# Softmax attention by pairs of heads: the minimum taken in the pass that adds the bias, and the 1/sum applied by a diagonal matrix in the turning product

## The chip, the cores and the metric

The kernel runs on one core of a Trainium2 chip. The metric is the time of one launch in microseconds of the device, lower is better. One core has a matrix engine (TensorE, "PE" in the profile, with its weight loads as "PEld"), a vector engine (VectorE, "DVE"), a scalar engine (ScalarE, "ACT"), GpSimd ("POOL") and a queue engine (SyncE, "SP") that issues the transfers. TensorE writes its products to PSUM, eight banks of 512 float32 per partition. All data here are float32.

## The reference, cut to what matters

The network has three blocks one after the other over a sequence of 512 tokens of width 1024. Two of them hold an attention that the change touches. In both, eight heads of 64 channels attend, and what is computed per head is

```
s = (q . k) * 64**-0.5 + bias          # bias: mask of chosen keys, or position table and window
p = exp(s - max(s)) / sum(exp(s - max(s)))
o = p @ v
```

In the first block (`dsa_sparse_attention`) a query may use 128 keys that an index score selects: the bias is 0 or -1e30, the same for every head. In the second (`na_attention`) a query of a 64 wide grid sees a window of neighbours (logits with a position table `rpb`, outside the window -1e30) and 256 context tokens without a bias:

```
s_loc = einsum(q * 64**-0.5, k_band) + bias ; s_loc = where(col_valid, s_loc, -1e30)
s_ctx = einsum(q * 64**-0.5, k_ctx)
p = softmax(concat([s_loc, s_ctx]))
```

## The kernel before, in words

The program is a row of blocks; in each, every engine has its own list of instructions, and semaphores order them. `Line` records an instruction of the vector or scalar engine and waits for its end before the next. `project` runs the tiles of a matrix product and, between them, what `Beside` has been given: `tensor_beside`, `scalar_beside` and `vector_beside` hold parts that each engine carries out behind the tile of that number (a number with a half: in the middle of that tile, on TensorE only).

`PairAttention` works on 16 pairs. A pair is two heads (a = 0, 1, partitions 0 to 63 and 64 to 127) by one block s of 128 queries, j = 0..3 outside and s = 0..3 inside. Step i of each engine is:

- TensorE (`tensor`): the score products of pair i+1 (`score`, L1542), which wait until both biased copies of pair i have left PSUM (`softened`) and the plain columns too; then the turning of pair i-2, head 0 (`turn`, L1553): its probabilities, 128 queries by `cols` keys, are transposed in blocks of 128 by 128 into one shared set of PSUM banks; then the products with the values of pair i-3 (`values`, L1567); then the turning of pair i-2, head 1, which needs the banks back (`copied`).
- VectorE (`vector`): for each head the copy `S = -scale * scores - bias` (L1594); for each head the minimum over the row of S (L1599); then for both heads of pair i-1 the reciprocal of the sum (L1606) and the probabilities times it, in place (L1607). Every fourth pair `close` takes the finished output (L1745 or L1936).
- ScalarE (`scalar`): `scale_plain` of pair i+1 (L1621: the columns without a bias, second block only); then for each head the copy of the turned probabilities of pair i-2 from PSUM (L1636) and the exponential of pair i with its sum (L1640), which waits for the minimum (`taken_max`).

In the first block (`dsa_attention`) block s has 128(s+1) keys, all with a bias, and the steps stand beside a product of 8 tiles (L454; each tile two halves of two matmuls of 512 columns). Of the steps, 0 and 1 stand ahead of the first tile, then two per tile. VectorE takes each finished tile out of PSUM (L1777) before the next steps. In the second block (`neighbourhood_attention`) each pair has 768 keys: 512 with a bias, 256 plain; there are no tiles beside it, but the last part of a convolution norm (`conv_norm`: L1869, L1876 on TensorE, L1882 to L1889 on VectorE, L1894 to L1903 on ScalarE) stands ahead of steps 0 to 7. There, ahead of every fourth pair, `prepare` (L1933) adds the window mask to two tables of 896 columns.

## Time and profile before

| | |
|---|---|
| median of 3 runs | 3554.92 us (3551.9 to 3556.33) |
| the profiled execution | 3554.84 us |
| its span in the profile | 3553.1 us |
| attention of the first block | 637.5 to 729.6 us of the span |
| attention of the second block | 1079.5 to 1201.0 us of the span |
| busy in the span | PE 3238.5 us, DVE 1517.0, ACT 723.8 |

All times of the profile are counted from the start of the span; the execution's own time has 1.7 us more than the span. PEclk in a view is the granted clock of TensorE: 1.00 is 2.4 GHz, 0.50 is 1.2 GHz. An "idle before" is put down to the instruction that ended it; "issue" means that the profile shows no such instruction. A busy time of PE is modelled, since matmuls overlap: from one start to the next is what an instruction occupies.

### The profile page before, as it was taken

The page shows a single profiled execution, that of the slowest core. Times are in us where ns is not written, and L with a number is a line of the kernel's source. Part 1 is how long each engine was busy: PE and PEld are TensorE (multiplying, and loading weights), DVE is VectorE, ACT ScalarE, POOL GpSimd, SP SyncE. Part 2 cuts the span into 40 slices and gives each one's busy share as a digit, 9 for nine tenths or more (in the row PEclk, how much of TensorE's full clock was granted, in tenths as well). Part 3 has the DMA queues.
Part 4 walks back from the last instruction along what each step waited for, and adds up shares of the span by engine and source line. Part 5 has one row for each costly group of instructions (what it writes and reads, how often), then busy time and mean ns, then how long its engine had stood idle before and what let it go on. Part 6 is the DMA issues. An engine that isn't in the chain of part 4 may idle for free. (4 is left out here: it accounts for less than half of the span.)

```text
span 3553.1 us, 39646 instructions
## 1 busy us (share of the span) xinstructions
PE 3238.5 (91%) x16518; PEld 1859.7 (52%) x16518; DVE 1517.0 (43%) x2332; ACT 723.8 (20%) x1110; POOL 0.2 (0%) x4
## 2 busy tenths in 40 slices
PE   7988989799897879999989898899998999999997
PEld 3476635344354533323232322687555886878874
DVE  2563146712296432222222221545443757475652
ACT  2210232311105410000000000100521332231403
POOL 0000000000000000000000000000000000000000
PEclk9998999899998989999999999999999999999998
DMA  7201033123211069999999999122211211221210
GB/s 257 95 3 64 32 108 136 48 95 131 82 48 55 25 255 428 427 428 428 427 428 428 427 428 414 70 72 89 76 48 48 71 66 54 72 72 48 72 47 24
DMA packets 120307, 588.36 MB, mean 166 GB/s; under 512 B 8897, under 2 KB 11073, under 8 KB 95425
## 3 DMA queue, kind: packets, MB, share of 16 engines
q1 hardware_dynamic: 120128, 585.83, 41.4%
q8 instruction: 131, 2.15, 0.2%
q14 instruction: 48, 0.39, 0.0%
HBM read 583.72 MB, written 2.10 MB: 165 GB/s over the span
## 5 line engine op out<-in xcount | busy, mean ns | idle before, releaser
L454 PE MATMUL ps<-hT,weight_ring 128*128 128x512 f32 x1216 | 544.3, 605 | 28.3 <-ACT hT L593 8.8
L454 PE MATMUL ps<-work,weight_ring 128*128 128x512 f32 (+1 forms) x960 | 426.9, 594 | 18.3 <-PEq L2675 8.3
L454 PEld LDWEIGHTS ps<-hT,weight_ring 128*128 128x128 f32 x1216 | 232.7, 194 | 316.8 <-issue 305.4
L454 PEld LDWEIGHTS ps<-work,weight_ring 128*128 128x128 f32 x960 | 182.0, 195 | 216.2 <-issue 205.5
L2248 PE MATMUL ps<-weight_ring,work 128*64 128x512 f32 x944 | 214.3, 597 | 32.3 <-DMA weight_ring<-in_w_up 19.7
L326 DVE TENSOR_TENSOR work<-work,ps 128x512 f32<-128x512 f32 x196 | 134.7, 687 | 248.7 <-PE ps L441 244.0
L441 PE MATMUL ps<-weight_ring 128*128 128x256 f32 x896 | 202.7, 379 | 0.0
L2378 DVE SCALAR_TENSOR_TENSOR xT<-ps,mod,xT 128x512 f32<-128x512 f32 x128 | 96.1, 751 | 224.4 <-PE ps L2266 222.0
L441 PE MATMUL ps<-hT,weight_ring 128*128 128x256 f32 x704 | 165.3, 392 | 19.5 <-DVE hT L602 15.6
L441 PEld LDWEIGHTS ps<-weight_ring 128*128 128x128 f32 x896 | 169.7, 190 | 24.7 <-issue 1.9
L2248 PE MATMUL ps<-work 128*64 128x512 f32 x672 | 153.3, 598 | 14.9 <-DMA work<-in_w_up 13.5
L441 PE MATMUL ps<-weight_ring,spare_slot 128*128 128x256 f32 x704 | 159.7, 380 | 3.7 <-DVE weight_ring L292 3.7
L441 PEld LDWEIGHTS ps<-hT,weight_ring 128*128 128x128 f32 x704 | 136.9, 196 | 41.9 <-issue 21.8
L2248 PEld LDWEIGHTS ps<-weight_ring,work 128*64 128x64 f32 x944 | 65.5, 136 | 174.7 <-issue 127.9
L441 PEld LDWEIGHTS ps<-weight_ring,spare_slot 128*128 128x128 f32 x704 | 133.0, 190 | 23.7 <-issue 5.9
L2373 DVE TENSOR_TENSOR work<-work,ps 128x512 f32<-128x512 f32 x32 | 33.9, 1060 | 191.8 <-PE ps L2248 191.3
L2393 DVE COPY work<-ps 128x512 f32<-128x512 f32 x16 | 11.1, 692 | 235.9 <-PE ps L2302 235.9
L2248 PEld LDWEIGHTS ps<-work 128*64 128x64 f32 x672 | 46.3, 136 | 116.1 <-issue 86.0
L2302 PE MATMUL ps<-weight_ring,work 128*64 128x512 f32 x448 | 100.3, 595 | 5.6 <-DMA weight_ring<-in_w_down 3.7
L545 ACT COPY work<-ps 128x512 f32<-128x512 f32 (+1 forms) x45 | 24.6, 547 | 395.3 <-PE ps L454 207.8
L2553 DVE TENSOR_TENSOR xT<-ps,xT 128x512 f32<-128x512 f32 x48 | 33.2, 692 | 158.1 <-PE ps L454 157.9
L2328 ACT ACTIVATE work<-ps 128x512 f32<-128x512 f32 x32 | 19.1, 597 | 385.5 <-PE ps L2248 385.0
(395 smaller groups left out, 4206.7 us busy)
## 6 DMA issues: line engine op xcount, KB each, us to landing
weight_ring<-in_w_gate SPq DMA_DIRECT2D x34, 2048.0 KB, 40.3
weight_ring<-in_w_down SPq DMA_DIRECT2D x28, 2048.0 KB, 40.2
work<-in_w_up SPq DMA_DIRECT2D x27, 2048.0 KB, 38.9
weight_ring<-in_w_up SPq DMA_DIRECT2D x25, 2048.0 KB, 38.2
work<-in_w_down SPq DMA_DIRECT2D x21, 2048.0 KB, 40.3
weight_ring<-in_w_in_odd SPq DMA_DIRECT2D x20, 2048.0 KB, 7.8
weight_ring<-in_w_in SPq DMA_DIRECT2D x18, 2048.0 KB, 9.0
work<-in_w_gate SPq DMA_DIRECT2D x15, 2048.0 KB, 40.2
```

Of the source, the lines that this page charges most:

```text
L326: v(dve.tensor_tensor(out, x, got, op), sig if out is steps[-1][0] else None)
L441: ins = pe.matmul(bank[:, j * L:(j + 1) * L], st, mv, start=k == 0, stop=k == 3)
L454: ins = pe.matmul(bank[0:m, 0:f], w[:, k, where:where + m], src[:, k, 0:ntok], start=k == 0, stop=k == kt - 1)
L545: return (lambda a, act, ps, sig: a(act.copy(out, ps), sig), None)
L2248: ins = pe.matmul(ps[64 * h:64 * h + 64, 1 + 2 * u + n, :], xs[:, 2 * (i % 2) + t, i // 2, :], w[:, t, c0:c0 + 512], start=i == 0 and t == ...
L2302: ins = pe.matmul(ps[64 * q:64 * q + 64, 7, :], hidT[:, i // 2, t, i % 2, :], w[:, t, q * 512:(q + 1) * 512], start=i == 0 and t == 0, sto ...
L2328: a(act.activation(sil[:, p, :], ps[:, 1 + p, :], ACT.Silu), silus)
L2373: v(dve.tensor_tensor(by_tile(hid[:, p, :]), strided(sil[:, p, :]), strided(ps[:, 3 + p, :]), MUL), hid_ready)
L2378: v(dve.scalar_tensor_tensor(ch.xT[:, n, :], ps[:, scatter_banks(e, i // 2)[i % 2], :], ch.mod2[:, 40 + n, 0:1], ch.xT[:, n, :], MUL, ADD) ...
L2393: v(dve.tensor_copy(y, ps[:, 7, :]), y_ready)
L2553: v(dve.tensor_tensor(ch.xT[:, n, :], ps, ch.xT[:, n, :], ADD), sig)
```

## The change

Three things are changed, in both attentions:

- The biased copy and the minimum are one instruction, `tensor_tensor_reduce`: `S = (scores + bias) * -scale` and the minimum of it, started from a given value. Where there are plain columns, their minimum is taken first, by a reduce over 256 columns, and is that start value; so the biased copy now comes behind `plain_scaled`. The exponential waits for `softened`; `taken_max` is gone.
- The probabilities are not multiplied in place any more. The reciprocals are multiplied into the identity matrix, 128 by 128, one of four diagonals; and the turning is an ordinary matmul with the unscaled exponentials as the stationary and that diagonal as the moving operand, in place of `transpose`. Before a diagonal is written again, VectorE waits for the turning of two pairs earlier (`turned`).
- The bias is now added ahead of the scaling, so the tables of the second block are multiplied by 8 when `prepare` adds the mask: `scalar_tensor_tensor` for `tensor_tensor`. The mask of the first block stays as it is (-1e30 becomes -1.25e29).

```diff
--- before.py
+++ after.py
@@ -1505,15 +1505,16 @@
 
 
 
-    def __init__(self, ch, pairs, scale, bank, width, rooms, cols):
+    def __init__(self, ch, pairs, scale, bank, width, rooms, cols, diagonals):
         self.ch, self.pairs, self.scale, self.width, self.bank = ch, pairs, scale, width, bank
+        self.diagonal = [diagonals[:, n * P:(n + 1) * P] for n in range(4)]
         self.turn_bank, self.value_bank = bank + 2 * width, bank + 3 * width
         pieces = [x[:, n:n + cols] for x in rooms for n in range(0, x.shape[1] - cols + 1, cols)]
         self.S, self.pT = pieces[0:8], pieces[8:12]
         self.st = ch.sm[:, 96:120].rearrange("p (i c) -> p i c", c=4)
-        (self.scores, self.softened, self.taken_max, self.expd, self.normed, self.turned, self.copied,
+        (self.scores, self.softened, self.expd, self.normed, self.turned, self.copied,
          self.summed, self.taken, self.plain_scaled) = ch.counters(
-            "scores", "scores_scaled", "maxima_ready", "exps_done", "probs_normed", "probs_turned",
+            "scores", "scores_scaled", "exps_done", "probs_normed", "probs_turned",
             "probs_copied", "values_summed", "group_taken", "plain_scaled")
         self.N = len(pairs)
         self.turns = self.N + 5
@@ -1550,8 +1551,8 @@
             if 2 * i + a >= 1:
                 pe.wait_ge(self.copied.sem, self.copied.at(2 * i + a))
             for t in range(self.pairs[i]["cols"] // P):
-                ins = pe.transpose(self.turn_banks()[:, t * P:(t + 1) * P],
-                                   self.S[2 * (i % 4) + a][:, t * P:(t + 1) * P], self.ch.m("ident"))
+                ins = pe.matmul(self.turn_banks()[:, t * P:(t + 1) * P], self.S[2 * (i % 4) + a][:, t * P:(t + 1) * P],
+                                self.diagonal[2 * (i % 2) + a], start=True, stop=True)
             ins.then_inc(self.turned.sem, 1)
             self.turned.total += 1
 
@@ -1591,20 +1592,22 @@
                     u["prepare"](v, dve)
                 for a in range(2):
                     b, w = u["bias"][a], u["biased"]
-                    v(dve.scalar_tensor_tensor(self.S[2 * (i % 4) + a][:, 0:w], self.score_banks(a)[:, 0:w], -self.scale, b,
-                                               MUL, SUB), self.softened)
-                for a in range(2):
+                    S, least = self.S[2 * (i % 4) + a], self.st[:, 2 * (i % 3) + a, 0:2]
                     if u["plain"]:
                         v.after(self.plain_scaled, 2 * i + a + 1)
-                    v(dve.tensor_reduce(self.st[:, 2 * (i % 3) + a, 1:2], self.S[2 * (i % 4) + a][:, 0:u["cols"]], AXX, MIN),
-                      self.taken_max)
+                        v(dve.tensor_reduce(least[:, 0:1], S[:, w:u["cols"]], AXX, MIN))
+                    v(dve.tensor_tensor_reduce(S[:, 0:w], self.score_banks(a)[:, 0:w], b, -self.scale,
+                                               least[:, 0:1] if u["plain"] else 3e38, ADD, MIN, least[:, 1:2]), self.softened)
             if 1 <= i < self.N + 1:
                 j = i - 1
                 for a in range(2):
-                    stat, x = self.st[:, 2 * (j % 3) + a, :], self.S[2 * (j % 4) + a][:, 0:self.pairs[j]["cols"]]
+                    stat = self.st[:, 2 * (j % 3) + a, :]
                     v.after(self.expd, 2 * j + a + 1)
                     v(dve.reciprocal(stat[:, 3:4], stat[:, 2:3]))
-                    v(dve.tensor_scalar(x, x, stat[:, 3:4], None, MUL), self.normed)
+                    if j >= 2:
+                        v.after(self.turned, 2 * j + a - 3)
+                    v(dve.tensor_scalar(self.diagonal[2 * (j % 2) + a], self.ch.m("ident"), stat[:, 3:4], None, MUL),
+                      self.normed)
             if i >= 5 and self.pairs[i - 5]["close"] is not None:
                 v.after(self.summed, i - 4)
                 self.pairs[i - 5]["close"](v, dve, self.ch.ps[:, self.value_bank + self.group[i - 5] % 2, :], self.taken)
@@ -1636,7 +1639,7 @@
                     line(act.copy(self.pT[2 * (j % 2) + a][:, 0:n], self.turn_banks()[:, 0:n]), self.copied)
                 if i < self.N:
                     x, stat = self.S[2 * (i % 4) + a][:, 0:self.pairs[i]["cols"]], self.st[:, 2 * (i % 3) + a, :]
-                    line.after(self.taken_max, 2 * i + a + 1)
+                    line.after(self.softened, 2 * i + a + 1)
                     line(act.activation(x, x, ACT.Exp, bias=stat[:, 1:2], scale=-1.0, accum_out=stat[:, 2:3]), self.expd)
         return part
 
@@ -1749,7 +1752,8 @@
                 v=[[v[:, t, (2 * j + a) * HD:(2 * j + a + 1) * HD] for t in range(s + 1)] for a in range(2)],
                 col=s * P, close=close if s == 3 else None))
     beside = Beside()
-    att = PairAttention(ch, pairs, HD ** -0.5, 3, 1, [ch.slot(0, 2).rearrange("p k t -> p (k t)"), ch.spare[:, :]], T)
+    att = PairAttention(ch, pairs, HD ** -0.5, 3, 1, [ch.slot(0, 2).rearrange("p k t -> p (k t)"), ch.spare[:, :]], T,
+                        ch.spare[:, 4 * T:5 * T])
     att.spread(beside, [-1] * 2 + halves(0, 8))
     beside.project(ch, 2, tiles, banks=3)
 
@@ -1930,7 +1934,8 @@
             for h in (2 * j, 2 * j + 1):
                 line.after(loaded, 16 * (h + 1))
                 t = tab[h % 4].rearrange("p (r c) -> p r c", c=64)
-                line(dve.tensor_tensor(t, t, ch.m("win")[:, 0:64].unsqueeze(1).to_broadcast([P, 14, 64]), ADD))
+                line(dve.scalar_tensor_tensor(t, t, HD ** 0.5, ch.m("win")[:, 0:64].unsqueeze(1).to_broadcast([P, 14, 64]),
+                                              MUL, ADD))
 
         def close(line, dve, ps, sig, j=j):
             line(dve.tensor_copy(out[:, j, :], ps), sig)
@@ -1942,7 +1947,9 @@
                 plain=(512, 256), cols=768,
                 v=[[v[:, t, (2 * j + a) * HD:(2 * j + a + 1) * HD] for t in range(6)] for a in range(2)],
                 col=s * P, close=close if s == 3 else None, prepare=prepare if s == 0 else None))
-    att = PairAttention(ch, pairs, HD ** -0.5, 0, 2, [ch.hT[:, :, :].rearrange("p k t -> p (k t)"), ch.spare[:, :], ch.slot(11).rearrange("p k t -> p (k t)")], 768)
+    att = PairAttention(ch, pairs, HD ** -0.5, 0, 2, [ch.hT[:, :, :].rearrange("p k t -> p (k t)"), ch.spare[:, :],
+                                                     ch.slot(11).rearrange("p k t -> p (k t)")], 768,
+                        ch.slot(11).rearrange("p k t -> p (k t)")[:, 1536:2048])
     (total, square_total), (square, take_root, finish), (centre, scale), rooted = conv_norm(
         ch, y, ch.slot(5), ch.slot(6), 7)
 
```

## Rows read from the trace of the kernel before

**Rows 1.** The page, part 1: busy time, share, instructions.

```profile
PE 3238.5 (91%) x16518; PEld 1859.7 (52%) x16518; DVE 1517.0 (43%) x2332; ACT 723.8 (20%) x1110; POOL 0.2 (0%) x4
```

**Rows 2.** Busy by stretch: length, PE, PEld, DVE, ACT, POOL; PEclk; DMA share, GB/s.

```profile
1079.48:1084.82 5.34, 1.57 (x10) 0.69 (x9) 3.59 (x5) 0.77 (x2) 0.00 (x0) 0.86 0.61 231
1084.82:1106.50 21.68, 14.02 (x44) 6.44 (x44) 19.91 (x31) 13.87 (x25) 0.00 (x0) 0.64 0.14 43
1106.50:1146.21 39.71, 27.65 (x221) 18.74 (x220) 27.96 (x43) 31.57 (x49) 0.00 (x0) 0.87 0.12 35
1146.21:1180.71 34.50, 27.79 (x264) 19.53 (x265) 32.71 (x53) 25.36 (x48) 0.00 (x0) 1.00 0.01 2
1180.71:1201.02 20.31, 15.50 (x176) 12.24 (x176) 11.26 (x20) 12.68 (x21) 0.00 (x0) 1.00 0.00 1
637.50:729.56 92.06, 73.14 (x368) 35.59 (x368) 57.18 (x140) 35.83 (x97) 0.00 (x0) 0.90 0.12 40
```

**Rows 3.** Timeline of one pair, TensorE: start, us, instruction, idle before.

```profile
1157.20 1.56 PE L1542 MATMUL ps<-work 64*128 64x512 f32 x8 [0.50 <-DVE spare_slot L1594]
1158.69 0.88 PE L1553 MATMUL ps<-masks,hT 128*128 128x128 f32 x6
1159.50 1.53 PE L1567 MATMUL ps<-work 128*64 128x128 f32 x24
1160.96 0.87 PE L1553 MATMUL ps<-masks,hT 128*128 128x128 f32 x6
1162.34 0.70 PE L1542 MATMUL ps<-work 64*128 64x512 f32 x2 [0.50 <-DVE spare_slot L1594]
```

**Rows 4.** Timeline of the same pair, ScalarE.

```profile
1159.69 0.80 ACT L1636 COPY spare_slot<-ps 128x768 f32<-128x768 f32 x1
1160.52 0.94 ACT L1640 ACTIVATE hT<-hT,small 128x768 f32<-128x768 f32 x1
```

**Rows 5.** Timeline of the third block, TensorE: 16 transposes.

```profile
2791.78 1.91 PE L2783 MATMUL ps<-masks,work 128*128 128x128 f32 x16
2793.53 0.81 PE L441 MATMUL ps<-spare_slot,weight_ring 128*128 128x256 f32 x3
```

**Rows 6.** Timeline of the third block, weight loads: 8 ordinary products.

```profile
2855.38 1.86 PEld L2815 LDWEIGHTS ps<-work 128*128 128x128 f32 x16 [0.49 <-DVE work L2766]
2857.16 0.73 PEld L441 LDWEIGHTS ps<-weight_ring 128*128 128x128 f32 x4
```

**Rows 7.** Groups by line and form, VectorE.

```profile
L2891 DVE TENSOR_TENSOR_SCAN work<-work 128x512 f32<-128x512 f32 x32 | 39.2, 1224 | 11.6 <-ACT work L2853 10.7
...
L1599 DVE TENSOR_REDUCE small<-hT 128x1 f32<-128x768 f32 x20 | 19.1, 953 | 0.7
...
L1594 DVE SCALAR_TENSOR_TENSOR hT<-ps,work 128x512 f32<-128x512 f32 x20 | 13.8, 691 | 0.7
...
L1607 DVE TENSOR_SCALAR hT<-hT,small 128x768 f32<-128x768 f32 x20 | 12.4, 620 | 0.7
...
L1933 DVE TENSOR_TENSOR work<-work,masks 128x896 f32<-128x896 f32 x8 | 8.7, 1092 | 20.3 <-PE ps L1542 18.0 <-DMA work<-in_rpb 2.2
...
L1712 DVE SCALAR_TENSOR_TENSOR work<-work,small 128x512 f32<-128x512 f32 x7 | 5.3, 752 | 0.2
...
L1599 DVE TENSOR_REDUCE small<-work 128x1 f32<-128x256 f32 x8 | 3.4, 420 | 0.3
...
L2131 DVE TENSOR_SCALAR work<-masks,small 128x128 f32<-128x128 f32 x8 | 2.3, 287 | 2.5 <-PEq L394 2.2
...
L903 DVE SCALAR_TENSOR_TENSOR work<-work 128x2048 f32<-128x2048 f32 x1 | 2.3, 2292 | 0.0
```

**Rows 8.** Timeline behind a tile of the first block, VectorE and TensorE.

```profile
672.58 0.69 DVE L1777 TENSOR_TENSOR work<-ps,work 128x512 f32<-128x512 f32 x1 [3.67 <-PE ps L454]
673.30 1.42 DVE L1594 SCALAR_TENSOR_TENSOR work<-ps,work 128x512 f32<-128x512 f32 x2
...
674.77 0.49 PE L1542 MATMUL ps<-work 64*128 64x128 f32 x4 [2.30 <-DVE work L1594]
```

## The prediction

> **What bounds the kernel now.** I read the page first: TensorE is busy in 91% of the span, VectorE in 43% [rows 1]. So a gain on VectorE counts only in stretches where TensorE waits for it. The change touches two: the attention of the first block (92.1 us, VectorE busy 57.2, TensorE 73.1) and that of the second (121.5 us from its first scores to its last close) [rows 2]. I cut the second at the starts of score products: opening (5.34 us), the half clock part (21.7), the part beside the convolution norm (39.7), the undisturbed pairs 9 to 15 (34.5), the drain behind the last scores (20.3) [rows 2].
>
> Then the timeline of one undisturbed pair. It takes 5.13 us, and VectorE fills it: two copies of 0.69, two minima of 0.95 and two scalings of 0.62 are 4.52 [rows 7], two reciprocals and the gaps the other 0.6. But TensorE waits only 0.50 us of it: 1.49 us of scores, 0.81 of the first turning, 1.46 of values, the second turning, each from start to start [rows 3]. ScalarE too is nearly full (per head a copy of 0.80, an exponential of 0.94 and its sum [rows 4]). Relief on VectorE can give at most 0.5 us per pair before TensorE is the limit.
>
> In the first block TensorE waits at another place: behind each tile, 2.30 us until VectorE has evicted the tile (0.69) and made two biased copies (1.42) [rows 8]. The minimum comes behind these, so that removing it shortens nothing there.
>
> **The turning product.** This is the large term. The third block has both kinds of instruction at 128 by 128. The 16 transposes of one step occupy TensorE for 1.75 us, 0.109 each [rows 5]. The 8 ordinary products of one step show as 16 pairs of load and matmul, 1.78 us to the next load, 0.111 each [rows 6]: an ordinary float32 product is two passes, a transpose one. The same doubling shows in this attention, where the 12 value products of a pair are 24 instructions and the 6 transposes are 6 [rows 3]. So a turned block goes from 0.109 to 0.222, +0.113 us. Turning one head of the second block (6 blocks) goes from 0.81 to 1.49 us. Bounds: 0, if the product with a diagonal went in one pass, and 0.135, if the 0.81 doubled as a whole.
>
> The second block turns 16 x 2 x 6 = 192 blocks (21.7 us more work), the first 4 x 2 x (1+2+3+4) = 80 (9.0 us). How much lands on the path:
> - Pairs 9 to 15: TensorE needs 1.49 + 1.49 + 1.46 + 1.49 = 5.93 us, and becomes the limit. VectorE's own list falls to 2 x (0.42 + 0.81 + 0.29) and the 0.6 for reciprocals and gaps, some 3.7. The six periods are three of 5.13, two of 5.86 (a close, 0.69 and its gap, on top) and one of 7.39 (two `prepare` of 1.09 and gaps on top), which is the stretch's 34.50. Five become 5.93: 29.65 for 27.11, +2.5. The one with `prepare` stays on VectorE: 2.6 + 2.25 + 2 x (0.45 + 0.85) = 7.5 (below), +0.15.
> - Drain: eight turnings stand behind the last score product, nothing of VectorE hides them: 8 x 0.68 = +5.5.
> - Beside the convolution norm: ten turnings, 6.8 us, but the stretch has ScalarE busy 31.6 of 39.7 and TensorE only 27.7 [rows 2]; where TensorE waits for ScalarE's table loads and copies, two passes hide. Its five periods, walked through the waits with these durations, come to 42.2 us: +2.5 (bounds 0 and 6.8).
> - Half clock part: two turnings, up to 2.8 us at half clock, and VectorE, busy 19.9 of the 21.7 us [rows 2], loses three pairs' minima there; what is left is between -2 and +2.8, and I take +0.75.
> - First block: TensorE goes without a pause from one turning to the next product, so all 9.0 us land. The removed minimum gives back 1.0 us at two turnings in the last pairs that waited for VectorE.
>
> **The fused copy and minimum.** No `tensor_tensor_reduce` stands in the trace. Nearest below: the plain two-operand pass, 0.691 for 512 columns. Nearest above: the scan, where each element needs the one before, 1.224 (two cycles per element), and in between a pass with a per-partition scalar, 0.752 [rows 7]. I take 0.81 (the scalar pass and 0.06 for putting the minimum out), +0.12 per instruction. On the path it counts twice per tile in the first block, 7 x 2 x 0.12 = +1.7. In undisturbed pairs of the second it does not: VectorE's next copies stand behind the diagonal of the pair before, and that behind ScalarE's copy (0.80) of the last turning and an exponential (0.94, its sum) [rows 4], 2.6 us behind the start of the scores; then 2 x (0.45 + 0.85), 5.2 in all, under 5.93. It would bind from 1.15 us per instruction on.
>
> The new wait for `plain_scaled` puts ScalarE's 0.38 and the 0.42 reduce [rows 7] ahead of each biased copy, and behind it are the two copies, the score products of the next pair and all of TensorE's list. In undisturbed pairs that is inside the 5.2 above. In the opening and in pairs with `prepare` it is on the path: opening 2 x 0.45 + 2 x 0.12 = +1.15.
>
> The diagonal costs 0.287 by the same operation of the router [rows 7], for 0.62 (0.29 to 0.49 in the first block). Its wait for the turning two pairs earlier costs nothing: the exponential ahead of it on ScalarE stands behind the copy of that same turning. If that cover went, VectorE would stand until the end of TensorE's list, and `copy and minimum` of the next pair with it.
>
> `prepare` becomes a three-operand pass over two tiles of SBUF. The row of that kind takes 2.292 us for 2048 columns, one cycle per element, as the add does: 1.09 stays [rows 7]. The Trainium skill (Vector Engine (DVE) Microarchitecture Reference, Points that are easy to get wrong) says that such a pass with two float32 sources in SBUF has half the throughput. By it, the four pairs with `prepare` would each be 1.9 us longer and the sum 7.5 more; the row speaks against it.
>
> **Sum.** Second block 1.15 + 0.75 + 2.5 + 2.65 + 5.5 = 12.55. First block 9.0 - 1.0 + 1.7 = 9.7. Together +22.3 on the profiled 3554.84, hence 3577; that execution is 0.1 below the median, so nothing is to be converted. Nothing behind takes it up: the experts' weights are fetched into slots that TensorE frees, and it frees them later.
>
> **Rivals.**
> - Clock relief. The half clock covers 20% of the first block's stretch and 26% of the one beside the norm (clock 0.90 and 0.87) [rows 2], some 18 and 10 us, in gaps of TensorE. With double turnings it may stay up, except in the cold starts: about 9 us and 10 us at half clock would give up to 4.5 and 1 to 2 us. Time 3571. Against it: the longest gaps (2.3 us behind each tile; table loads) stay. The Trainium skill (TensorE: Matmul & The Clock Gate, Part 4: PE-mode transpose) says that transposes do not count as activity, which speaks for this rival. The undisturbed pairs, full of transposes, hold 1.00 [rows 2], so it decides little.
> - The fused pass is slow, at the scan's 1.22: +0.53 instead of +0.12 on 14 instructions of the first block's path (+5.7), and +3.4 in the second: 3586.
> - The diagonal product takes one pass. Then the second block stays (VectorE's gain of 0.5 in undisturbed pairs against the later copies), the first gains 1.0 and loses 1.7: 3555, no change.
> - Faster: TensorE has room, so that VectorE's relief decides. A pair falls from 5.13 to 4.6 us, 13 pairs by 0.5, and nothing is lost in the first block: 3548. It decides as long as a turned block costs under 0.04 us more (0.5 us of slack over 12 blocks); [rows 5, 6] say 0.113.
>
> **Numbers.** Forecast (two passes on the path) 0.70, clock relief 0.12, slow fused pass 0.10, one pass 0.04, faster 0.04. Range: from clock relief with a fused pass at 0.69 (3571 less 5, 3566) to the slow pass with a little unhidden loading (3588). No change is within 0.2% (7.1 us), about what a measurement can tell. Faster 0.04, same 0.05, slower 0.91.
>
> **What would show it.** L1553 should have 544 records for 272, 0.11 us apart; undisturbed pairs 5.9 us long with TensorE at no wait for VectorE; the drain 26 us; the first block's stretch 102 us with the waits behind tiles at 2.5 us; VectorE's busy time down by some 38 us (23.7 in the second block, 15 in the first). It is wrong if L1553 shows single passes, if the fused pass takes over 1.15 us, or if the clock's share differs much.

## The result and the profile after

The changed kernel takes 3584.31 us (median of 4 executions, 3580.07 to 3586.26) against 3553.41 for the kernel before (4 executions): ratio 1.0085, 95% interval 1.0073 to 1.0098. It is slower by under 1%, 30.9 us by the medians, and the interval excludes no change. A second set of four executions gave 3582.01 against 3552.78, ratio 1.0081 (1.0067 to 1.0095). The profiled execution, the fastest of its four, took 3580.07 us, 25.2 more than the profiled one of before. The forecast was 3577 (3566 to 3588).

The page of the changed kernel, busy time by engine, against [rows 1]:

```profile
PE 3272.2 (91%) x16790; PEld 1895.4 (53%) x16790; DVE 1473.4 (41%) x2364; ACT 724.3 (20%) x1110; POOL 0.2 (0%) x4
```

VectorE is relieved of 43.6 us, TensorE has 33.7 more and 272 instructions more: the doubled turnings. So work was taken from an engine that was busy in 43% of the span and given to one that is busy in 91%.

The changed kernel by stretch, cut at the same events as [rows 2] (starts of score products; last close of each attention), in the same order and with the same columns (the first block's scores start at 637.60 us in both kernels, so that its 101.64 us stand against 91.96):

```profile
1086.63:1093.01 6.38, 1.56 (x9) 0.69 (x9) 4.57 (x9) 0.77 (x2) 0.00 (x0) 1.00 0.69 254
1093.01:1116.77 23.76, 16.07 (x57) 8.66 (x57) 13.23 (x35) 13.88 (x25) 0.00 (x0) 0.64 0.12 31
1116.77:1160.00 43.23, 34.67 (x281) 26.54 (x280) 22.56 (x55) 30.26 (x48) 0.00 (x0) 0.88 0.09 27
1160.00:1197.51 37.51, 36.20 (x336) 28.84 (x337) 23.57 (x66) 26.28 (x48) 0.00 (x0) 1.00 0.01 2
1197.51:1223.66 26.15, 21.34 (x225) 18.45 (x224) 5.99 (x18) 13.10 (x21) 0.00 (x0) 1.00 0.01 1
637.60:739.24 101.64, 84.71 (x448) 48.15 (x448) 38.70 (x140) 35.82 (x97) 0.00 (x0) 0.89 0.11 39
```

Every stretch is longer: opening +1.04, half clock part +2.08, beside the norm +3.52, pairs 9 to 15 +3.01, drain +5.84, together +15.5 in the second block. The first block is 9.7 us longer. In pairs 9 to 15 TensorE is now busy 36.2 of 37.5 us, VectorE 23.6 instead of 32.7.

The timeline of one pair of the changed kernel, TensorE, against [rows 3]:

```profile
1160.00 1.56 PE L1543 MATMUL ps<-work 64*128 64x512 f32 x8 [0.35 <-DVE small L1599]
1161.49 1.60 PE L1554 MATMUL ps<-work,hT 128*128 128x128 f32 x12
1163.03 1.53 PE L1568 MATMUL ps<-work 128*64 128x128 f32 x24
1164.49 1.60 PE L1554 MATMUL ps<-work,spare_slot 128*128 128x128 f32 x12
1166.02 0.70 PE L1543 MATMUL ps<-work 64*128 64x512 f32 x2
```

Each turning has 12 records for 6 and takes 1.53 to 1.54 us from its start to the next, where it took 0.81. The pair is 6.02 us long and the last line has no wait in front of it: TensorE is the limit.

The groups of VectorE by line and form over the second attention of the changed kernel (busy us, mean ns | idle before), against [rows 7]:

```profile
L1599 DVE CUSTOM_DVE_ANT_0 hT<-ps,work,small 128x512 f32<-128x512 f32 x20 | 15.0, 751 | 0.7
...
L1937 DVE SCALAR_TENSOR_TENSOR work<-work,masks 128x896 f32<-128x896 f32 x8 | 8.7, 1093 | 20.7 <-PE ps L1543 20.4
L1598 DVE TENSOR_REDUCE small<-hT 128x1 f32<-128x256 f32 x20 | 8.4, 420 | 5.1 <-ACT hT L1624 4.5
L1606 DVE RECIPROCAL small<-small 128x1 f32<-128x1 f32 x32 | 5.2, 164 | 33.5 <-ACT hT L1643 17.1 <-ACT spare_slot L1643 15.9
L1598 DVE TENSOR_REDUCE small<-spare_slot 128x1 f32<-128x256 f32 x12 | 5.0, 420 | 7.5 <-ACT spare_slot L1624 7.2
...
L1599 DVE DVE_READ_ACCUMULATOR2_ANT small<- 128x1 f32 x32 | 2.7, 84 | 0.0
```

The fused instruction shows as two: the pass, 751 ns, and an accumulator read of 84. VectorE's saved time turned into waiting: 33.5 us ahead of the reciprocals (for the exponentials; 6.8 before), and 11.7 us ahead of the plain columns' reduce, for ScalarE's copy of them, where the minimum of the whole row waited 2.8 before. The first block starts its minimum from a constant; its groups there:

```profile
L1609 DVE TENSOR_SCALAR spare_slot<-masks,small 128x128 f32<-128x128 f32 x32 | 9.2, 287 | 1.4 <-DVE small L1606 0.3
...
L1599 DVE CUSTOM_DVE_ANT_0 work<-ps,work 128x512 f32<-128x512 f32 x8 | 5.5, 692 | 0.3
```

So the pass costs as much as the plain two-operand pass (691), and a seed read from SBUF 60 ns more. The timeline behind a tile of the first block, VectorE and TensorE, against [rows 8]:

```profile
677.14 0.69 DVE L1781 TENSOR_TENSOR work<-ps,work 128x512 f32<-128x512 f32 x1 [4.58 <-PE ps L454]
677.87 0.69 DVE L1599 CUSTOM_DVE_ANT_0 work<-ps,work 128x512 f32<-128x512 f32 x1
678.49 0.08 DVE L1599 DVE_READ_ACCUMULATOR2_ANT small<- 128x1 f32 x1
678.60 0.69 DVE L1599 CUSTOM_DVE_ANT_0 work<-ps,work 128x512 f32<-128x512 f32 x1
...
679.36 0.49 PE L1543 MATMUL ps<-work 64*128 64x128 f32 x4 [2.32 <-DVE small L1599]
```

Here the read lies inside the pass's own end, the next pass starts 0.73 us behind the first, and TensorE waits 2.32 us where it waited 2.30.

**The rest of the 25.2.** Between the two attentions 2.5 us come back (349.9 to 347.4 us from close to first scores). Behind the second, one stretch differs, around the router. Its rows, from the last `L2000` (`L2007` in the changed kernel) to the first expert's gated hidden values (L2373, L2380), of the kernel before:

```profile
1262.00:1332.30 70.30, 52.25 (x266) 25.17 (x266) 28.86 (x72) 14.60 (x21) 0.00 (x0) 0.85 0.77 322
```

and of the changed one:

```profile
1284.60:1357.90 73.30, 54.61 (x266) 24.30 (x266) 28.86 (x71) 14.61 (x21) 0.00 (x0) 0.81 0.74 308
```

TensorE's same 266 instructions are busy 2.4 us longer at a mean granted clock of 0.81 for 0.85, and the stretch is 3.0 us longer. 9.7 - 2.5 + 15.5 + 3.0 is 25.7, and the rest of the program is some 0.4 shorter.

### The profile page after: what moved, and what is told of

It reads as the page before. It is cut to its first block and busy times, and to the rows that moved or that the text cites. A ratio compares the mean times of both kernels' runs of the same rounds, so it can differ in the third digit from the quotient of the medians.

```text
span 3578.3 us, 40275 instructions
## 1 busy us (share of the span) xinstructions
PE 3272.2 (91%) x16790; PEld 1895.4 (53%) x16790; DVE 1473.4 (41%) x2364; ACT 724.3 (20%) x1110; POOL 0.2 (0%) x4
## 5 line engine op out<-in xcount | busy, mean ns | idle before, releaser
L441 PEld LDWEIGHTS ps<-weight_ring 128*128 128x128 f32 x896 | 169.7, 190 | 24.7 <-issue 1.9
L441 PEld LDWEIGHTS ps<-weight_ring,spare_slot 128*128 128x128 f32 x704 | 133.0, 190 | 24.7 <-issue 6.8
L2380 DVE TENSOR_TENSOR work<-work,ps 128x512 f32<-128x512 f32 x32 | 34.0, 1062 | 191.7 <-PE ps L2255 191.2
L545 ACT COPY work<-ps 128x512 f32<-128x512 f32 (+1 forms) x45 | 24.7, 548 | 395.0 <-PE ps L454 207.4
```

The costliest lines, as they stand in the source:

```text
L441: ins = pe.matmul(bank[:, j * L:(j + 1) * L], st, mv, start=k == 0, stop=k == 3)
L545: return (lambda a, act, ps, sig: a(act.copy(out, ps), sig), None)
L2380: v(dve.tensor_tensor(by_tile(hid[:, p, :]), strided(sil[:, p, :]), strided(ps[:, 3 + p, :]), MUL), hid_ready)
```

## The experiments

Each was timed against the kernel before. The stretches are from one profiled execution each; the first block's varies by some 3 us with the share of half clock alone (the runs with the fused pass alone and with the late minimum have the same instructions there: 87.9 us at clock 0.93, 90.8 at 0.89), the second's hardly (137.03 and 137.06 us in two executions of the changed kernel). Outside the two attentions the instructions are the same in all of these kernels, and yet the thirteen profiled executions differ there: the first attention's first scores start between 635.2 and 642.9 us of the span, and from the second attention's last close to the end it takes 2348.7 to 2358.2 us. So the total of a single execution places nothing; the stretches do, and the medians say what a change costs in all.

| kernel | median us | ratio to before, 95% | second attention us | first attention us |
|---|---|---|---|---|
| before | 3552.56 to 3553.41 | | 121.54 | 91.96 |
| changed | 3584.31 and 3582.01 | 1.0085, 1.0081 | 137.03 | 101.64 |
| transposes | 3553.13 | 1.0003 (0.9994 to 1.0011) | 125.60 | 87.67 |
| diagonal only | 3577.24 | 1.0065 (1.0053 to 1.0077) | 132.22 | 99.98 |
| fused only | 3558.08 | 1.0013 (1.0004 to 1.0021) | 127.13 | 87.86 |
| late minimum | 3550.32 | 0.9995 (0.9987 to 1.0004) | 116.42 | 90.84 |
| changed, late minimum | 3575.45 | 1.0062 (1.0048 to 1.0076) | 130.48 | 102.01 |
| transposes twice | 3571.69 | 1.0052 (1.0039 to 1.0065) | 131.03 | 99.82 |
| early steps | 3537.77 | 0.9958 (0.9946 to 0.9971) | 121.53 | 72.99 |
| late and early | 3537.51 | 0.9954 (0.9941 to 0.9966) | 118.46 | 73.43 |
| changed, early steps | 3564.97 | 1.0035 (1.0022 to 1.0049) | 137.03 | 83.66 |
| first block only | 3563.24 | 1.0028 (1.0018 to 1.0039) | 121.33 | 100.57 |

**Transposes in the changed kernel.** This one leaves out the 1/sum: the diagonals are made, but nothing uses them. It answers for time only.

```diff
-                ins = pe.matmul(self.turn_banks()[:, t * P:(t + 1) * P], self.S[2 * (i % 4) + a][:, t * P:(t + 1) * P],
-                                self.diagonal[2 * (i % 2) + a], start=True, stop=True)
+                ins = pe.transpose(self.turn_banks()[:, t * P:(t + 1) * P],
+                                   self.S[2 * (i % 4) + a][:, t * P:(t + 1) * P], self.ch.m("ident"))
```

> The changed kernel with one edit: the turning is the transpose against the identity again; the diagonals are still made, but unused, so the probabilities are left without their 1/sum. Theory A (the two passes of the turning product on TensorE's path are the cost): the turning group has 272 records again, a pair falls from 6.02 to about 5.0 us or less, the drain from 26.2 to about 20.5, the first block's stretch from 101.6 to about 92.5; the time is 3550 to 3558, no change against the kernel before and 23 to 34 below the changed one. Rival B (the fused pass and its new wait ahead of the biased copy are the cost): it stays above 3570. Rival C (clock relief hides part of the two passes in the changed kernel): the difference to the changed kernel is under 20 us, with more of the time at half clock.

Measured 3553.13 us, no difference from the kernel before. One edit gives back all 30 us; theory A holds, B and C fall as the main cause. Its drain is 20.32 us long, as before. Its first attention is 87.67 us, 4.8 below what I had expected, with a mean clock of 0.93 for 0.90. One pair in its timeline of TensorE:

```profile
1175.47 1.56 PE L1543 MATMUL ps<-work 64*128 64x512 f32 x8
1176.96 0.87 PE L1554 MATMUL ps<-masks,spare_slot 128*128 128x128 f32 x6
1177.76 1.53 PE L1568 MATMUL ps<-spare_slot,work 128*64 128x128 f32 x24
1179.28 0.85 PE L1554 MATMUL ps<-masks,spare_slot 128*128 128x128 f32 x6
1180.61 1.56 PE L1543 MATMUL ps<-work 64*128 64x512 f32 x8 [0.48 <-DVE small L1599]
```

Turning 0.80, pair 5.14, and the wait for VectorE is back, though VectorE's list is far shorter than before (2.95 us busy in another such pair of 5.15): it waits itself, for ScalarE's exponentials, ahead of the copies that TensorE needs. The second attention is still 4.1 us longer than before (opening +1.04, half clock part +1.68, beside the norm +1.30). Against this kernel, the changed one has more of the full clock in the second attention (0.64 for 0.56 in the half clock part, 1.00 for 0.90 in pairs 9 to 15) and less in the first (0.89 for 0.93). So theory C's relief is there in part, and it doesn't come near to paying for the second passes.

**The diagonal alone.** The kernel before, with only these edits (and the place of the four diagonals, as in the changed kernel):

```diff
-                ins = pe.transpose(self.turn_banks()[:, t * P:(t + 1) * P],
-                                   self.S[2 * (i % 4) + a][:, t * P:(t + 1) * P], self.ch.m("ident"))
+                ins = pe.matmul(self.turn_banks()[:, t * P:(t + 1) * P], self.S[2 * (i % 4) + a][:, t * P:(t + 1) * P],
+                                self.diagonal[2 * (i % 2) + a], start=True, stop=True)
...
-                    v(dve.tensor_scalar(x, x, stat[:, 3:4], None, MUL), self.normed)
+                    if j >= 2:
+                        v.after(self.turned, 2 * j + a - 3)
+                    v(dve.tensor_scalar(self.diagonal[2 * (j % 2) + a], self.ch.m("ident"), stat[:, 3:4], None, MUL),
+                      self.normed)
```

> The kernel before with one part of the change: the reciprocals go into diagonals and the turning is the product with them; copy, minimum and bias tables stay as before. Theory A: nearly the whole loss is here, 19 us over the kernel before by the walk through both attentions (10.6 in the second, 8.4 in the first), so 3570 to 3578; the pair about 6 us, as in the changed kernel. Rival B (the fused pass with its wait is the cost): at most 10 us over the kernel before, under 3564.

Measured 24.7 us over the kernel before, inside the interval of theory A and more than the 19 walked. The second attention is 10.7 us longer, of which the drain alone is 5.84 (26.15 us, as in the changed kernel), the first 8.0: together the 19 walked. The other 6 us of the medians are not in the attentions of this profile; its router stretch has 3 of them (73.3 us for 70.3), outside what the edit touches, and the rest isn't placed.

**The fused pass alone.** Transposes (by the edit of the run above that has them in the changed kernel) and the scaling in place, the rest as changed:

```diff
-                    stat = self.st[:, 2 * (j % 3) + a, :]
+                    stat, x = self.st[:, 2 * (j % 3) + a, :], self.S[2 * (j % 4) + a][:, 0:self.pairs[j]["cols"]]
...
-                    if j >= 2:
-                        v.after(self.turned, 2 * j + a - 3)
-                    v(dve.tensor_scalar(self.diagonal[2 * (j % 2) + a], self.ch.m("ident"), stat[:, 3:4], None, MUL),
-                      self.normed)
+                    v(dve.tensor_scalar(x, x, stat[:, 3:4], None, MUL), self.normed)
```

> The other part alone: the copy keeps its minimum (with the plain columns' reduce ahead of it), the probabilities are scaled in place and turned by transposes. Theory A: the 14 minima saved in the first block lie off the path and the fused pass is 0.08 us longer twice per tile; in the second block the later copies cost what the shorter list gives: 3551 to 3556, no change. Rival B (fused pass and wait cost): 10 us or more over the kernel before, over 3563. Rival D (VectorE was the limit of the second block's pairs, and its relief shows once TensorE has room): pairs of about 4.7 us, 3545 to 3549.

Measured 3558.08: 5.5 us over, ratio 1.0013 with an interval that excludes 1. I had expected no change; this part costs something too, though less than rival B says. The two parts alone add up: 24.7 + 5.5 = 30.2, the changed kernel has 29 to 31. Rival D's faster kernel is not to be seen. Its second attention is 5.6 us longer (127.13; the first is 4.1 us shorter in this profile and 1.1 in that of the next run, at a lower clock), and the groups of VectorE there say why:

```profile
L1598 DVE TENSOR_REDUCE small<-hT 128x1 f32<-128x256 f32 x20 | 8.4, 420 | 5.9 <-ACT hT L1621 5.4
...
L1598 DVE TENSOR_REDUCE small<-spare_slot 128x1 f32<-128x256 f32 x12 | 5.0, 421 | 7.0 <-ACT spare_slot L1621 6.7
```

12.9 us of idle time stand ahead of the plain reduce, 12.1 of them waiting for ScalarE's plain copy; the biased copy, the next scores and all of TensorE's list are behind it.

**Late minimum.** As the last, but that wait and reduce are put behind both biased copies:

```diff
-                    S, least = self.S[2 * (i % 4) + a], self.st[:, 2 * (i % 3) + a, 0:2]
-                    if u["plain"]:
-                        v.after(self.plain_scaled, 2 * i + a + 1)
-                        v(dve.tensor_reduce(least[:, 0:1], S[:, w:u["cols"]], AXX, MIN))
-                    v(dve.tensor_tensor_reduce(S[:, 0:w], self.score_banks(a)[:, 0:w], b, -self.scale,
-                                               least[:, 0:1] if u["plain"] else 3e38, ADD, MIN, least[:, 1:2]), self.softened)
+                    least, start = self.st[:, 2 * (i % 3) + a, 1:2], self.st[:, 2 * (i % 3) + a, 0:1]
+                    v(dve.tensor_tensor_reduce(self.S[2 * (i % 4) + a][:, 0:w], self.score_banks(a)[:, 0:w], b, -self.scale,
+                                               3e38, ADD, MIN, start if u["plain"] else least), self.softened)
+                for a in range(2):
+                    least, start = self.st[:, 2 * (i % 3) + a, 1:2], self.st[:, 2 * (i % 3) + a, 0:1]
+                    if u["plain"]:
+                        x = self.S[2 * (i % 4) + a][:, u["biased"]:u["cols"]]
+                        v.after(self.plain_scaled, 2 * i + a + 1)
+                        v(dve.tensor_tensor_reduce(x, x, x, 0.5, start, ADD, MIN, least), self.plain_least)
...
-                    line.after(self.softened, 2 * i + a + 1)
+                    line.after(self.plain_least if self.pairs[i]["plain"] else self.softened, 2 * i + a + 1)
```

> As the run with the fused pass alone, but the biased copy does not wait for the plain columns: it starts its minimum from a constant, and the plain columns' minimum is taken behind both copies in a pass started from the first minimum, which does nothing else of use. If the new wait ahead of the biased copy is what eats the gain of the shorter VectorE list in the second block: 3 to 6 us below the kernel before, 3547 to 3551, pairs of about 4.75 us. If the wait costs nothing there (ScalarE's plain copy is in time in any case): the same as the fused pass alone within 1.5 us.

Measured 3550.32, 7.8 us below the fused pass alone, and its second attention is 10.7 shorter than that one's and 5.1 shorter than before. The VectorE groups of this kernel:

```profile
L1603 DVE CUSTOM_DVE_ANT_0 hT<-hT,small 128x256 f32<-128x256 f32 x20 | 9.7, 485 | 0.7
...
L1603 DVE CUSTOM_DVE_ANT_0 spare_slot<-spare_slot,small 128x256 f32<-128x256 f32 x12 | 5.8, 485 | 3.3 <-ACT spare_slot L1624 2.8
```

The idle time falls from 12.9 to 4.0 us, though this pass is longer than the reduce (485 and a read, for 420). Three of its four undisturbed pairs take 4.6 us (the other 4.96) where they took 5.13: with one pass on TensorE and the wait out of the way, the 0.5 us per pair that VectorE's relief can give is there. Against the kernel before the time is not different (0.9987 to 1.0004), 2.2 us less by the medians; the rest of the 5.1 us is lost outside the second attention. The profiled execution, 5.6 us above this kernel's median, has a router stretch of 73.3 us too.

**The changed kernel with the late minimum.** The same edit on the changed kernel.

> The changed kernel with one edit: the biased copy does not wait for the plain columns, whose minimum is taken behind both copies, as in the run with the late minimum. Theory A (two causes: the second pass of the turning product, about 24 us, and the wait for the plain columns in the first nine pairs of the second block, 4 to 6): 4 to 7 us below the changed kernel, 3576 to 3581, opening 5.3 us again and the part beside the norm 2 to 3 us shorter, the undisturbed pairs still 6.02. Rival (TensorE bound by two passes hides that wait too): the same as the changed kernel within 1.5 us.

Measured 3575.45, ratio 1.0062 where the changed kernel has 1.0085 and 1.0081, so some 7 to 9 us less. That TensorE's two passes hide the wait falls. By stages it is below the changed kernel by 1.04 in the opening, 1.82 in the half clock part, 2.66 beside the norm, 1.03 in pairs 9 to 15 (all in the one with `prepare`) and 0 in the drain, 6.55 in sum. The undisturbed pairs stay at 6.02. The two middle stages also have more of the full clock in this execution (0.77 for 0.64, 0.92 for 0.88), so that their 4.5 us are wait and clock together; VectorE's idle time ahead of the plain pass is 4.3 us for 12.6.

**Transposes twice.** The kernel before, each transpose issued twice to the same place:

```diff
             for t in range(self.pairs[i]["cols"] // P):
-                ins = pe.transpose(self.turn_banks()[:, t * P:(t + 1) * P],
-                                   self.S[2 * (i % 4) + a][:, t * P:(t + 1) * P], self.ch.m("ident"))
+                for _ in range(2):
+                    ins = pe.transpose(self.turn_banks()[:, t * P:(t + 1) * P],
+                                       self.S[2 * (i % 4) + a][:, t * P:(t + 1) * P], self.ch.m("ident"))
```

> The kernel before with one edit: each of the 272 transposes of the turning is issued twice, to the same place; all of VectorE and ScalarE stays. Theory A (only TensorE's second pass costs, whatever it computes): as the run with the diagonals alone, 22 to 27 us over the kernel before, 3574 to 3580, pairs of about 5.9 to 6.1 us. Rival (something of the diagonal itself costs: its wait, its place in VectorE's list, or that an ordinary product is slower than a transpose): under 18 us over, below 3571.

Measured 18.5 us over: between the two bands, so my figure was too high and the rival's no more than touched. The point is that doubling TensorE's passes, with nothing of VectorE changed, costs 18.5 of the 24.7 us; in the two attentions alone it is 17.3 of 18.7. Its timeline shows the pair, 5.88 us long:

```profile
1158.43 1.56 PE L1542 MATMUL ps<-work 64*128 64x512 f32 x8
1159.93 1.53 PE L1554 MATMUL ps<-masks,hT 128*128 128x128 f32 x12
1161.39 1.53 PE L1568 MATMUL ps<-work 128*64 128x128 f32 x24
1162.85 1.53 PE L1554 MATMUL ps<-masks,spare_slot 128*128 128x128 f32 x12
1164.31 1.56 PE L1542 MATMUL ps<-work 64*128 64x512 f32 x8
```

Twelve transposes take 1.46 us, twelve passes of the product 1.53 to 1.54. Over the drain's eight turnings that is 25.55 against 26.15 us. Both attentions together differ by 1.4 us from the diagonal alone; of the other 5 us, 3 are in the router stretch (70.3 for 73.3 us), outside what either edit touches, and the rest I can't place.

**Early steps.** The kernel before; in the first block VectorE's step is put ahead of the eviction of a tile:

```diff
-    def spread(self, beside, places):
+    def spread(self, beside, places, early=0):
...
-            beside.add(places[min(i, len(places) - 1)], self.tensor(i), self.scalar(i), self.vector(i))
+            where = places[min(i, len(places) - 1)]
+            beside.add(where, self.tensor(i), self.scalar(i))
+            beside.add(max(-1, where - early if i < len(places) else where), vector=self.vector(i))
...
-    att.spread(beside, [-1] * 2 + halves(0, 8))
+    att.spread(beside, [-1] * 2 + halves(0, 8), early=0.5)
```

> The kernel before with one edit in the first block: VectorE's step stands ahead of the eviction of a tile and not behind it, so that the biased copies do not wait for the eviction; 7 waits of 2.3 us behind tiles get shorter by up to 2 each. Theory A: 10 to 15 us below the kernel before, 3538 to 3543, with no wait of TensorE for L1594 behind a tile over 0.5 us. Rival: the tile's PSUM bank comes free later and TensorE waits for it instead: within 3 us of the kernel before.

Measured 15.4 us below the kernel before, just beyond the better end. The group of score products between 637 and 740 us, first of the kernel before:

```profile
L1542 PE MATMUL ps<-work 64*128 64x128 f32 (+3 forms) x64 | 14.8, 545 | 20.1 <-DVE work L1594 14.0 <-PEq L394 6.1
```

then with early steps:

```profile
L1542 PE MATMUL ps<-work 64*128 64x128 f32 (+3 forms) x64 | 14.5, 534 | 7.9 <-PEq L394 6.1 <-DVE work L1594 1.8
```

The wait for VectorE falls by 12.2 us. Behind tiles none is left: the 1.8 us stand ahead of the first tile, and no wait of TensorE for a tile's bank came in their place. The attention itself gets 19.0 us shorter; with the shorter waits goes a half clock that covers less of it (mean 0.94 for 0.90), and which share is the clock's no run separates. 1.8 us go again ahead of the second attention.

**Late minimum and early steps together.** Both edits above.

> Late minimum with transposes, and the early steps of the first block together. If they are independent: the sum of both runs, 12 to 19 us below the kernel before, 3534 to 3541, the fastest of all. If the early steps need VectorE's time that the late minimum has moved: no better than the early steps alone.

Measured 3537.51, 15.7 us below before; no measurable gain over the early steps alone, though its second attention is 3.1 us shorter. Both beat the two kernels of this case; the early steps alone are the smaller edit.

**The changed kernel again.** No edit.

> The changed kernel once more, beside the others of this call, because its four executions gave 30.9 us over the kernel before and its profiled one 25.2. By the profiles (first block +9.7, second +15.5) it should be 25 to 28 over. If 30 or more again, 5 us lie outside the two attentions.

Measured 29.2 us over, above the 25 to 28 that the profiles gave, its profiled execution (3577.7) again the fastest of four (to 3587.4). The granted clocks of the four, from the fastest to the slowest, are 0.969, 0.968, 0.967 and 0.966: its slower executions have more half clock. That goes with the 4 to 5 us between medians and profiles, and the runs show no more than that.

**The changed kernel with early steps.** Edit as above.

> The changed kernel with the early steps of the first block. If the second passes of the first block fill TensorE's waits behind tiles once VectorE's copies are no longer behind the eviction, the early steps give less than the 15.4 they give before the change: 8 to 15 us below the changed kernel, 3568 to 3574. If the two are independent: 15 or 16 below it, so 3564 to 3568 (the two passes still cost all of their 9 us there).

Measured 3564.97, 17.0 us below the changed kernel timed beside it, its first attention 18.0 shorter, about as much as the 19.0 before the change. The two are independent: the second pass didn't go into the waits behind tiles, nor does it now.

**The change in the first block only.** The second attention runs through the code of before, `prepare` and its tables too. The edit, without the class `WholePairs` that holds that code:

```diff
-    att = PairAttention(ch, pairs, HD ** -0.5, 0, 2, [ch.hT[:, :, :].rearrange("p k t -> p (k t)"), ch.spare[:, :],
-                                                     ch.slot(11).rearrange("p k t -> p (k t)")], 768,
-                        ch.slot(11).rearrange("p k t -> p (k t)")[:, 1536:2048])
+    att = WholePairs(ch, pairs, HD ** -0.5, 0, 2, [ch.hT[:, :, :].rearrange("p k t -> p (k t)"), ch.spare[:, :], ch.slot(11).rearrange("p k t -> p (k t)")], 768)
```

> The change in the first block's attention alone, the second as before. By the forecast's split: 9 to 12 us over the kernel before, 3562 to 3565, and the second block's stretch 121.5 us. Rival (loss in the first block is taken up on the way to the second, which started only 7.2 us later in the changed kernel): 5 to 8 over, 3558 to 3561.

Measured 10.5 us over, second attention 121.3: the forecast's share. The loss isn't taken up on the way: 0.9 us of it comes back between the attentions.

## Why the prediction was right

The forecast case, two passes on TensorE's path, is what happened; the time is 7 us above its figure and inside the range. Of the 7, the two attentions have 3 (25.2 for 22.3); the other 4 are what the median of this kernel has over its profiled execution. By its steps:

- **The turning product.** L1554 has 544 records, so that the rival of one pass falls. Taken: 0.81 to 1.49 per turning. Measured: 1.53 to 1.54, +0.73 and not +0.68; the small term by which the drain (+5.84 for +5.5) and each undisturbed pair (6.02 for 5.93) are longer. The bound by doubling the 0.81 (1.62) was not reached.
- **Pairs 9 to 15.** +3.01 for +2.65. Five pairs of 6.02, and the one with `prepare` 7.40 where 7.5 was worked out.
- **The fused pass.** Taken 0.81; measured from pass to pass 0.73 with a constant start and 0.79 with a seed (VectorE: 0.42 reduce and pass come every 1.25 us, worked out as 1.30). In the first block the +1.7 us was too much: waits of TensorE for VectorE ahead of the scores went from 14.0 to 14.2 us. The slow pass is refuted, at 692 and 751 ns against the scan's 1224.
- **First block.** +9.7 for +9.7, but partly by luck. The fused pass costs 0.2 instead of 1.7, the turnings 80 x 0.122 = 9.8 instead of 9.0, and TensorE's waits ahead of turnings fall by 2.1 (3.3 to 1.2 us) where 1.0 was taken. That is 7.9; the rest goes with the mean clock, 0.89 for 0.90. Single executions of kernels with the second passes there lie between 99.8 and 102.0 us, so a match to a tenth means nothing.
- **The wait for the plain columns.** This step was mis-sized. The forecast put it on the path only in the opening (+1.15, measured +1.04) and in pairs with `prepare`. The late minimum in the changed kernel makes the half clock part 1.82 us shorter and the part beside the norm 2.66 as well (with the clock's share in it). VectorE stands there four times for the plain copy, 2.17, 2.57, 2.15 and 4.62 us. The last two, with what went ahead of them:

```profile
1134.28 2.93 PE L1543 MATMUL ps<-work 64*128 64x512 f32 x8 [1.14 <-DVE small L1599]
1137.31 0.38 ACT L1624 ACTIVATE hT<-ps 128x256 f32<-128x256 f32 x1 [2.23 <-issue]
1137.82 0.42 DVE L1598 TENSOR_REDUCE small<-hT 128x1 f32<-128x256 f32 x1 [2.15 <-ACT hT L1624]
...
1145.27 3.35 ACT L1907 ACTIVATE work<-work,vectors 128x512 f32<-128x512 f32 x4
1148.65 0.80 ACT L1624 ACTIVATE spare_slot<-ps 128x256 f32<-128x256 f32 x2
1149.17 0.42 DVE L1598 TENSOR_REDUCE small<-spare_slot 128x1 f32<-128x256 f32 x1 [4.62 <-ACT spare_slot L1624]
```

In the first three ScalarE is not late: it waits itself until the scores are done (2.93 us at the half clock), and then its plain copy and VectorE's reduces stand between the scores and the biased copies, as in the opening. Only in the fourth is ScalarE behind, with the norm's work (L1907). With the late minimum these two stages are only 0.3 and 0.9 us longer than before, less than the 0.75 and 2.5 worked out for them. In sum they are +5.6 for +3.25: the one step of the forecast that left out a wait, at two places.

- **The diagonal.** 287 ns; ahead of its 64 instructions VectorE stood idle 2.5 us in all, so that its wait for the older turning costs nothing, as worked out. VectorE's busy time fell by 25.5 us in the second attention and 18.5 in the first (23.7 and 15 worked out).
- **`prepare`.** 1093 ns for 1092. The rule cited of the Trainium skill (Vector Engine (DVE) Microarchitecture Reference, Points that are easy to get wrong), half the throughput for two float32 sources in SBUF, isn't borne out by this row.
- **Clock relief.** No relief against the kernel before: mean clock 0.64 and 0.88 in the half clock part and beside the norm (0.64 and 0.87 before), 0.89 for 0.90 in the first block, 0.81 for 0.85 around the router. That transposes don't count as activity, as the Trainium skill has it (TensorE: Matmul & The Clock Gate, Part 4: PE-mode transpose), could not be told from these rows: pairs 9 to 15 hold 1.00 with transposes (before) and with products (changed), but have 0.90, 0.90 and 0.95 in three runs with transposes (transposes in the changed kernel, fused only, late minimum), which nothing here explains.
- **Faster.** It falls with the time. That a pair can reach 4.6 us shows in the run with the late minimum, where a turned block is one pass.
- **Nothing behind takes it up.** Nearly: 2.5 us come back between the attentions and 3.0 are lost again around the router.

What stays open: the medians have 29 to 31 us where the profiled executions have 25.2 (and 22.9 for the second profiled one against the same execution of before). The half clock share goes with it, but which stretches hold it in the slower executions wasn't recorded.

Not tried: a transpose with the diagonal in the identity's place. No run shows whether it would scale what it turns, nor how many passes it would take.

## What to carry to other kernels

Scaling inside a product that replaces a float32 transpose isn't free: it doubled TensorE's passes, here 272 more of 0.12 us, to relieve an engine that TensorE waited for only 0.5 us per pair. Before a step is made shorter on the engine that seems full, read how long the other one really waits for it; and when two instructions are fused, look at what each of them waited for, since the fused one waits for both (here 7 to 9 us, given back by taking the plain minimum later). The largest gain of the case, 15.4 us, came from the place where TensorE did wait, and from order alone (the clock's share included): the step that releases it goes ahead of the eviction.

## What the runs showed of the hardware

- A 128 by 128 float32 product shows as two loads with a matmul each, a transpose as one (544 records and 272). One such pass of the product takes 0.128 us (12 in 1.535), one transpose 0.122 us when 12 stand in a row (1.46). The weight loads differ (ns: least, median, most), first in the changed kernel, then in the one with transposes twice:

```profile
L1554 PEld LDWEIGHTS ps<-work,hT x240: 186/192/333, 1108.1 to 1211.4; 128*128 128x128 f32 x120
```

```profile
L1554 PEld LDWEIGHTS ps<-masks,hT x240: 138/141/232, 1109.4 to 1208.0; 128*128 128x128 f32 x120
```

- A pass that also gives a minimum costs what the pass costs: 692 ns for 512 columns, 751 with the start value in SBUF, and an accumulator read of 83 to 84 ns that mostly lies in the gap.
- The share of the half clock moves in a stretch whose work hasn't changed, and its time with it: the router stretch took 68.9, 70.3, 71.7 or 73.3 us in the kernels here, at mean clocks of 0.88, 0.85, 0.83 and 0.81. What decides between these no run shows.
